# Attention over 96 units: the value products of two units side by side, and one copy of VectorE moved

## The chip, the cores and the metric

One core of a Trainium2 chip runs the whole layer as a single program. The metric is the time of one execution on the device in microseconds. Besides the DMA queues four engines do the work: TensorE (PE, with its weight loads PEld), VectorE (DVE), ScalarE (ACT) and GpSimd (POOL). Each runs its own list of instructions in order, and they wait for each other by semaphores.

## The reference

The reference is one layer of an encoder, on 1024 sample tokens and 512 prompt tokens. The change lies in the attention, of which there are two kinds with 8 heads of 64 each:

```python
# windowed, with a sink, per block of 128 queries and up to 3 blocks of keys
s = einsum(q, k) * HEAD_DIM ** -0.5           # masked to |i - j| <= 128
m = max(max(s), sink);  p = exp(s - m)
o = einsum(p / (sum(p) + exp(sink - m)), v)
# neighbourhood, 2-D, with a bias per relative position
s = einsum(q, k) * HEAD_DIM ** -0.5 + bias    # masked to the neighbourhood
o = einsum(softmax(s), v)
```

After it come a norm, the output projection, a router and 16 experts with SwiGLU.

## The kernel before, in words

The attention is the function `attend`. It works through 24 blocks of 128 queries: 12 of the windowed kind and 12 of the neighbourhood kind, mostly in turn. A block has four pairs of heads; a block and a pair are a **unit**, so there are 96 units. A unit has 384 keys in 16 of the blocks (64 units) and 256 keys in the other 8 (32 units).

A unit goes through a pipeline over several **steps**; each engine runs its own loop over u from 0 to 100, and in step u it works on different units:

- TensorE: scores of unit u for both heads (L886); then the probabilities of unit u-2 are transposed into `flip_ps` (L896, 4 small transposes per 128 keys); then the output of unit u-5 is transposed into `out_ps` (L907); and last the values of unit u-3 are multiplied into `mixed_ps` (L927), both heads beside each other in two halves of the array. All are fp32, so that a matmul is recorded as two.
- VectorE: for each head of unit u the mask or bias is added to the scores and their maximum taken (L809, the two **additions**); the maximum of both is negated (L817 or L820); for unit u-2 the reciprocal of the sum (L825) and the copy of one half of the transposed probabilities to `at_flipped` (L830, the **copy**); for unit u-5 the output is scaled by the reciprocal and written to `ld_out` (L845, the **scaling**).
- ScalarE: the copy of `mixed_ps` for unit u-4 to `at_o_turn` (L744, the **output copy**); the copy of the other half of the transposed probabilities of unit u-2 (L750); and the exponentials of unit u, one per head (L758).

Buffers are few, and the waits for them set the order: three banks for scores, one bank for `mixed_ps` (so the values of a unit wait until the output copy of the unit before has read it: `o_copied`), and one buffer `out_ps` for the turned output (so the turn of one unit waits until the scaling of the unit before has read it: `scaled`). SyncE moves biases and values in, and outputs out. In the last steps ScalarE also squares the first tile of outputs that has come back from memory (L767), for the stage that follows.

Of the kernel before, what the change touches and what calls it, by code (L numbers as in the profile page):

```python
# [24 lines left out]
ACT = mybir.ActivationFunctionType  # L25
# [3 lines left out]
P = 128  # L29
# [9 lines left out]
HD = 64  # L39
# [585 lines left out]
def attend(nc, d, keep, shared, lead):  # L625
# [4 lines left out]
    with ctx:  # L630
# [40 lines left out]
        def flip_from(v, i):  # L671
            tiles = units[v][0].keys // P
            return flip_ps[i][:, 0:2 * tiles * HD].rearrange("p (h c q) -> p h c q", h=2, q=HD)
# [62 lines left out]
        @block.scalar  # L736
        def _(act):
            for u in range(STEPS):
                v = u - WEIGH
                if 0 <= v < N:  # L740
                    act.wait_ge(weighed, v + 1)
                    if v >= 2:
                        act.wait_ge(o_turned, v - 1)
                    act.activation(o_turn[:, v % 2, :], mixed_ps[:, 0:P], ACT.Copy).then_inc(o_copied, 1)  # L744
                if 0 <= u - FLIP < N:
                    v = u - FLIP
                    act.wait_ge(flipped_ps, 2 * v + 1)
                    if 2 * v >= FLIPS:
                        act.wait_ge(weighed, v - FLIPS // 2 + 1)
                    act.activation(flip_to(v, 0), flip_from(v, 0), ACT.Copy).then_inc(copied[0], 1)  # L750
                if u < N:
                    b, r = units[u][0], u % STATS
                    act.wait_ge(bounded, u + 1)
                    if u >= PROBS // 2:
                        act.wait_ge(flipped_ps, 2 * (u - PROBS // 2) + 2)
                    pair, n = units[u][1], b.keys + b.window
                    for h in range(2):
                        act.activation(probs[:, (2 * u + h) % PROBS, 0:n],  # L758
                                       raw[:, 2 * pair + h, NEAR_KEYS - b.keys:NEAR_KEYS - b.keys + n],
                                       ACT.Exp, bias=neg_top[:, r, h:h + 1],  # L760
                                       accum_out=sums[:, r, h:h + 1]).then_inc(exped, 1)

                if u == N - 1 or u == N:
                    k = u - (N - 1)
                    if k == 0:
                        act.wait_ge(lead.o_in[0], 16)
                    act.activation(lead.merged[:, k * HALF:(k + 1) * HALF], lead.o[0][:, k * HALF:(k + 1) * HALF],  # L767
                                   ACT.Square, accum_out=lead.ss[:, k:k + 1]).then_inc(lead.squared, 1)
                if u == N + 2:
                    act.wait_ge(lead.squared, 2)  # L770
                    act.activation(lead.rt[:], lead.ss[:], ACT.Sqrt, bias=shared.eps[:],
                                   scale=1.0 / HALF).then_inc(lead.root, 1)

            def split(j):
                act.wait_ge(lead.w_in[j], 16)
                act.activation(lead.w_hi[j], lead.w[:, j, :], ACT.Copy,
                               scale=shared.gain_out[:, j:j + 1]).then_inc(lead.hi_w, 1)

            split(0)
            act.wait_ge(lead.refined, REFINE)  # L780
            for k in range(2):
                c = slice(k * HALF, (k + 1) * HALF)
                act.activation(lead.merged[:, c], lead.o[0][:, c], ACT.Copy,
                               scale=lead.rs[:, k:k + 1]).then_inc(lead.normed, 1)
            split(1)
            for k in range(2):
                act.wait_ge(lead.turned, k + 1)
                act.activation(lead.m_hi[:, 4 * k:4 * k + 4, :].rearrange("p j c -> p (j c)"), lead_ps[k][:],
                               ACT.Copy).then_inc(lead.hi_m, 1)

        @block.vector
        def _(dve):
            dve.wait_ge(shared.later_in, 48)
            dve.tensor_scalar(neg_sink[:], sink[:], -1.0, None, ALU.mult).then_inc(negated, 1)
            dve.tensor_copy(raw[:, :, NEAR_KEYS:], sink[:].unsqueeze(2)).then_inc(negated, 1)
            dve.wait_ge(negated, 2)
            for u in range(STEPS):
                if u < N:
                    b, pair, bi = units[u]
                    r = u % STATS  # L800
                    if not b.window and pair == 0:
                        dve.wait_ge(bias_in[b.number % BIASES], 16 * (b.number // BIASES + 1))
                    for h in range(2):
                        dve.wait_ge(scored, 2 * u + h + 1)
                        if b.window:
                            add = band[:, b.mask_at:b.mask_at + b.keys]
                        else:
                            add = bias[:, b.number % BIASES, 2 * pair + h, 0:b.keys]
                        dve.tensor_tensor_reduce(out=raw[:, 2 * pair + h, NEAR_KEYS - b.keys:NEAR_KEYS],  # L809
                                                 in0=score[(2 * u + h) % SCORES][:, 0:b.keys], in1=add, scale=1.0, scalar=-3.0e38,  # L810
                                                 op0=ALU.add, op1=ALU.max,
                                                 accum_out=top[:, r, h:h + 1]).then_inc(added, 1)
                    dve.wait_ge(added, 2 * u + 2)
                    if b.window:

                        mine = neg_sink[:, 2 * pair:2 * pair + 2]
                        dve.scalar_tensor_tensor(out=neg_top[:, r, :], in0=top[:, r, :], scalar=-1.0, in1=mine,  # L817
                                                 op0=ALU.mult, op1=ALU.min).then_inc(bounded, 1)
                    else:
                        dve.tensor_scalar(neg_top[:, r, :], top[:, r, :], -1.0, None,  # L820
                                          ALU.mult).then_inc(bounded, 1)
                if 0 <= u - FLIP < N:
                    v, r = u - FLIP, (u - FLIP) % STATS
                    dve.wait_ge(exped, 2 * v + 2)
                    dve.reciprocal(rden[:, r, :], sums[:, r, :]).then_inc(inverted, 1)  # L825

                    dve.wait_ge(flipped_ps, 2 * v + 2)
                    if 2 * v >= FLIPS:
                        dve.wait_ge(weighed, v - FLIPS // 2 + 1)
                    dve.tensor_copy(flip_to(v, 1), flip_from(v, 1)).then_inc(copied[1], 1)  # L830
                if u >= OUT:
                    v, r = u - OUT, (u - OUT) % STATS
                    b, pair, bi = units[v]
                    dve.wait_ge(o_turned, v + 1)
                    dve.wait_ge(inverted, v + 1)
                    if pair == 0 and bi >= O_SLOTS:

                        dve.wait_ge(stored[bi % O_SLOTS], 16 * (bi // O_SLOTS))
                    if b.window:
                        dst = o[:, bi % O_SLOTS, :].rearrange("p (h c e) -> p h c e", h=2, c=PAIRS)[:, :, pair, :]  # L840
                    else:
                        dst = o[:, bi % O_SLOTS, pair * P:(pair + 1) * P].rearrange("p (h e) -> p h e", h=2)

                    own = out_ps[:, :, 0:HD]
                    dve.tensor_tensor(dst, own,  # L845
                                      rden[:, r, :].unsqueeze(2).broadcast_to([P, 2, HD]),
                                      ALU.mult).then_inc(scaled, 1)
                if u == N + 3:
                    dve.wait_ge(lead.root, 1)
                    inverse_root(dve, lead.refined, 0, lead.ss[:], lead.rt[:], [lead.tmp[:, i, :] for i in range(3)],  # L850
                                 lead.rs[:], 1.0 / HALF)
# [17 lines left out]
        def _(pe):  # L869

            for u in range(STEPS):
# [30 lines left out]
                if u >= OUT:  # L902
# [4 lines left out]
                    turned = [nc.tensor.transpose(out_ps[:, h, 0:HD], o_turn[ROWS[h], v % 2, :],  # L907
                                                  ident[ROWS[h], ROWS[h]]) for h in range(2)]
                    turned[1].then_inc(o_turned, 1)
                for v in (u - WEIGH + 1,):  # L910
                    if 0 <= v < N:
                        b, pair, bi = units[v]
                        if not b.window and pair == 0:
                            pe.wait_ge(v_in[b.strip % 2], 16 * len(V_TILES) * (b.strip // 2 + 1))
                        if v >= 1:
                            pe.wait_ge(o_copied, v)
                        for h in range(2):
                            pe.wait_ge(copied[h], v + 1)
# [1 line left out]
                        for i in range(tiles):  # L920
                            for h in range(2):
                                if b.window:
                                    values = keep.v.tiles(b.first_key + i, 1)[:, 0, h * HD:(h + 1) * HD]
                                else:
                                    slot = (len(V_TILES) * b.strip + b.v_tiles[i]) % V_SLOTS
                                    values = v_near[:, slot, pair * P + h * HD:pair * P + (h + 1) * HD]
                                last = nc.tensor.matmul(mixed_ps[h * HD:(h + 1) * HD, 0:P], values,  # L927
                                                        flipped[:, (2 * v + h) % FLIPS, i * P:(i + 1) * P],
                                                        start=i == 0, stop=i == tiles - 1, tile_position=(0, h * HD))
                        last.then_inc(weighed, 1)  # L930
# [1129 lines left out]
```

## Time and profile before

| | us |
|---|---|
| median of 3 runs | 2554.14 (2553.98 to 2557.11) |
| the profiled execution's own time | 2556.15 |
| its span | 2554.4 |
| TensorE busy, of the span | 2462.6 |
| attention: first scores to last scaling | 327.4 to 541.6 |

TensorE is busy in 96% of the span, but that is a mean: in the attention it is the engine with most to do, beside VectorE and ScalarE that are busy for more than 80% of the time each. The experts, from about 760 us on, are most of the span and TensorE fills them. A row of the timeline merges neighbouring instructions of one kind; a bracket at its end tells how long its engine sat idle before, and who released it.

### The profile page before, as it was taken

How to read it: one execution, taken by the hardware profiler on the slowest of the kernel's cores; microseconds unless marked ns; L12 is line 12 of the kernel's file. 1: busy time of each engine (PE TensorE's matmuls, PEld its weight loads, DVE VectorE, ACT ScalarE, POOL GpSimd, SP SyncE). 2: the span in 40 equal slices, each digit the busy share in tenths (PEclk: the TensorE clock that was granted, in tenths of full speed). 3: DMA queues.
4: the chain of work that ended last, by engine and by line, in shares of the span. 5: the costliest groups of instructions: out<-in, count | busy, mean ns of one | idle time of the engine just before them, and what ended most of it. 6: DMA issues, size and time to landing. Idle time of an engine off the chain costs nothing.

```text
span 2554.4 us, 42578 instructions
## 1 busy us (share of the span) xinstructions
PE 2462.6 (96%) x16082; PEld 2204.3 (86%) x16082; DVE 1683.9 (66%) x2550; ACT 1475.4 (58%) x2081; POOL 159.2 (6%) x165
## 2 busy tenths in 40 slices
PE   8999999989949999999999999999999999999997
PEld 7888866667739899998989999898999989999896
DVE  6354278864577676666767667676766767676676
ACT  4333278877636555565655656555565655556574
POOL 0000000000010101010110101011010100101010
PEclk9999999989969999999999999999999999999999
DMA  5343254454437767676776767677676767767685
GB/s 186 111 140 112 66 176 133 138 188 143 146 143 256 241 241 252 218 258 227 253 242 242 245 227 253 225 258 244 237 243 229 255 223 257 245 233 249 229 320 212
DMA packets 99668, 542.37 MB, mean 212 GB/s; under 512 B 11072, under 2 KB 15552, under 8 KB 49408
## 3 DMA queue, kind: packets, MB, share of 16 engines
q1 hardware_dynamic: 92192, 515.30, 57.2%
q0 software_dynamic: 7392, 25.96, 4.5%
q8 instruction: 52, 0.85, 0.1%
q14 instruction: 32, 0.26, 0.0%
HBM read 500.32 MB, written 40.89 MB: 212 GB/s over the span
## 4 chain that ended last, share of the span: by engine, by line
PE 68%; DVE 2%; DMA 1%; ACT 1%; issue 0%; POOL 0%; DVEq 0%; SPq 0%; ACTq 0%; POOLq 0%
PE ex_gate_ps L1854 16%; PE ex_up_ps L1854 15%; PE ex_gate_ps L1856 7%; PE ex_up_ps L1856 7%; PE ex_up_ps L1868 2%; PE ex_down_ps L1868 2%; PE ex_down_ps L1869 2%; PE ex_down_ps L1870 2%; PE ex_down_ps L1871 2%; PE ex_up_ps L1870 2%; PE ex_down_ps L1872 2%; PE ex_up_ps L1872 2%; PE ex_up_ps L1869 2%; PE ex_up_ps L1871 2%; PE ex_turn_ps L1829 1%; PE ex_turn_ps L1831 0%
## 5 line engine op out<-in xcount | busy, mean ns | idle before, releaser
L1706 DVE TENSOR_TENSOR ex_w_lo<-ex_w,ex_w_hi 128x2048 fp32r<-128x2048 f32 x384 | 880.0, 2292 | 461.0 <-ACT ex_w_hi L1623 448.5
L1623 ACT ACTIVATE ex_w_hi<-ex_w 128x2048 fp32r<-128x2048 f32 x384 | 733.4, 1910 | 221.4 <-PE ex_down_ps L1872 106.9
L1854 PE MATMUL ex_gate_ps<-ex_xt,ex_w_hi 128*128 128x384 f32 x2048 | 594.2, 360 | 1.5 <-DVE ex_xt L1712 1.5
L1854 PE MATMUL ex_up_ps<-ex_xt,ex_w_hi 128*128 128x384 f32 x2048 | 592.1, 359 | 0.0
L1856 PE MATMUL ex_gate_ps<-ex_xt,ex_w_lo 128*128 128x192 f32 x2048 | 513.7, 251 | 0.0
L1856 PE MATMUL ex_up_ps<-ex_xt,ex_w_lo 128*128 128x192 f32 x2048 | 512.7, 250 | 0.0
L1856 PEld LDWEIGHTS ex_gate_ps<-ex_xt,ex_w_lo 128*128 128x128 f32 x2048 | 392.5, 192 | 0.6
L1856 PEld LDWEIGHTS ex_up_ps<-ex_xt,ex_w_lo 128*128 128x128 f32 x2048 | 391.2, 191 | 0.0
L1854 PEld LDWEIGHTS ex_gate_ps<-ex_xt,ex_w_hi 128*128 128x128 f32 x2048 | 385.8, 188 | 2.3 <-issue 1.7
L1854 PEld LDWEIGHTS ex_up_ps<-ex_xt,ex_w_hi 128*128 128x128 f32 x2048 | 384.4, 188 | 0.0
L1641 ACT ACTIVATE ex_gate_low<-ex_gate_ps 128x384 f32<-128x384 f32 x128 | 62.9, 491 | 208.4 <-PE ex_gate_ps L1856 207.1
L1643 ACT ACTIVATE ex_up_low<-ex_up_ps 128x384 f32<-128x384 f32 x128 | 62.8, 491 | 208.0 <-PE ex_up_ps L1856 208.0
L423 DVE TENSOR_TENSOR pj_w_lo<-pj_w,pj_w_hi 128x1024 fp32r<-128x1024 f32 x54 | 66.2, 1225 | 155.0 <-ACT pj_w_hi L343 154.7
L758 ACT ACTIVATE at_probs<-at_raw,at_neg_top 128x385 f32<-128x385 f32 (+3 forms) x192 | 110.0, 574 | 29.2 <-DVE at_neg_top L820 14.3
L1564 POOL DMA_INDIRECT acc_scratch<-ex_y_s,ex_scatter_s x15 | 24.2, 1612 | 1436.9 <-DVE ex_y_p L1749 1436.9
L1733 DVE TENSOR_TENSOR ex_up_sum<-ex_up_ps,ex_up_low 128x384 f32<-128x384 f32 x128 | 71.4, 557 | 50.5 <-ACT ex_up_low L1643 50.5
L1868 PE MATMUL ex_down_ps<-ex_w_hi,ex_ht 128*128 128x512 f32 x256 | 101.4, 396 | 0.0
L1868 PE MATMUL ex_up_ps<-ex_w_hi,ex_ht 128*128 128x512 f32 x256 | 101.3, 396 | 0.0
L1869 PE MATMUL ex_down_ps<-ex_w_lo,ex_ht 128*128 128x512 f32 x256 | 99.8, 390 | 0.0
L1871 PE MATMUL ex_down_ps<-ex_w_hi,ex_ht 128*128 128x512 f32 x256 | 99.8, 390 | 0.0
L1870 PE MATMUL ex_down_ps<-ex_w_hi,ex_ht 128*128 128x512 f32 x256 | 99.8, 390 | 0.0
L1870 PE MATMUL ex_up_ps<-ex_w_hi,ex_ht 128*128 128x512 f32 x256 | 99.7, 389 | 0.0
(316 smaller groups left out, 4056.1 us busy)
## 6 DMA issues: line engine op xcount, KB each, us to landing
ex_w<-in_w_experts SPq DMA_DIRECT2D x384, 1024.0 KB, 4.8
pj_w<-in_w_in SPq DMA_DIRECT2D x54, 512.0 KB, 3.6
at_bias<-in_near_bias SPq DMA_DIRECT2D x8, 1536.0 KB, 8.2
at_v_near<-v_scratch SPq DMA_DIRECT2D x24, 256.0 KB
o_scratch<-ld_out SPq DMA_DIRECT2D x24, 256.0 KB, 4.5
q_p<-in_x SPq DMA_DIRECT2D x12, 512.0 KB, 4.3
acc_scratch<-k_p SPq DMA_DIRECT2D x12, 512.0 KB, 5.1
h_scratch<-q_p SPq DMA_DIRECT2D x12, 512.0 KB, 2.9
```

What stands on the lines that cost most here:

```text
L423: dve.tensor_tensor(w_lo[:, i % W_SLOTS, :, :].rearrange("p j c -> p (j c)"), w[:, i % W_SLOTS, :], w_hi[:, i % W_SLOTS, :, :].rearrange(" ...
L758: act.activation(probs[:, (2 * u + h) % PROBS, 0:n], raw[:, 2 * pair + h, NEAR_KEYS - b.keys:NEAR_KEYS - b.keys + n], ACT.Exp, bias=neg_to ...
L1623: act.activation(w_hi[:, c % SLOTS, :], w[:, c % SLOTS, :], ACT.Copy).then_inc(hi_w, 1)
L1706: dve.tensor_tensor(w_lo[:, c % SLOTS, :], w[:, c % SLOTS, :], w_hi[:, c % SLOTS, :].bitcast(F32), ALU.subtract).then_inc(lo_w, 1)
L1733: dve.tensor_tensor(up_sum[:], up_ps[:, :, 0:CAP], up_low[:], ALU.add).then_inc(up_summed, 1)
L1854: nc.tensor.matmul(out[:, b, 0:2 * CAP], w_hi[:, slot, f], xt[:, k, :, :].rearrange("p h c -> p (h c)"), start=k == 0, stop=False)
L1856: last = nc.tensor.matmul(out[:, b, 0:CAP], w_lo[:, slot, f], xt[:, k, 0, :], start=False, stop=k == DT - 1)
L1868: nc.tensor.matmul(out[0], s_hi, hi, start=start, stop=False)
L1869: nc.tensor.matmul(out[0], s_hi, lo, start=False, stop=False)
L1870: nc.tensor.matmul(out[0], s_lo, hi, start=False, stop=stop)
L1871: nc.tensor.matmul(out[1], both, hi, start=start, stop=False)
L1872: last = nc.tensor.matmul(out[1], both, lo, start=False, stop=stop)
```

## The change

In every even step TensorE multiplies the values of two units, u-4 and u-3, one after the other into two ranges of columns of the one bank `mixed_ps`; in odd steps it multiplies none. ScalarE copies both outputs with one instruction, twice as wide, in every odd step. And in every odd step VectorE's copy of the transposed probabilities stands between the additions of the two heads, in place of behind the reciprocal. The last steps, which have no scores, keep the copy where it was.

```diff
+                if u % 2 and u > WEIGH:
+                    v = u - WEIGH - 1
+                    act.wait_ge(weighed, v + 2)
                     if v >= 2:
-                        act.wait_ge(o_turned, v - 1)
-                    act.activation(o_turn[:, v % 2, :], mixed_ps[:, 0:P], ACT.Copy).then_inc(o_copied, 1)
+                        act.wait_ge(o_turned, v)
+                    act.activation(o_turn[:].rearrange("p u c -> p (u c)"), mixed_ps[:, 0:2 * P],
+                                   ACT.Copy).then_inc(o_copied, 2)
...
+            def copy_turned(v):
+                dve.wait_ge(flipped_ps, 2 * v + 2)
+                if 2 * v >= FLIPS:
+                    dve.wait_ge(weighed, v - FLIPS // 2 + 1)
+                dve.tensor_copy(flip_to(v, 1), flip_from(v, 1)).then_inc(copied[1], 1)
...
+                        if h == 0 and u % 2 and u >= FLIP:
+                            copy_turned(u - FLIP)
...
-                    dve.tensor_copy(flip_to(v, 1), flip_from(v, 1)).then_inc(copied[1], 1)
+                    if u % 2 == 0 or u >= N:
+                        copy_turned(v)
...
-                for v in (u - WEIGH + 1,):
+                for v in (u - WEIGH, u - WEIGH + 1) if u % 2 == 0 else ():
...
-                        if v >= 1:
+                        if v >= 2 and v % 2 == 0:
                             pe.wait_ge(o_copied, v)
...
-                                last = nc.tensor.matmul(mixed_ps[h * HD:(h + 1) * HD, 0:P], values,
+                                last = nc.tensor.matmul(mixed_ps[h * HD:(h + 1) * HD, v % 2 * P:(v % 2 + 1) * P], values,
```

TensorE's list in the middle of the attention, before (two steps of 384 keys):

```order
L886 MATMUL at_score<-k_s,q_s 128x384 x2
L896 MATMUL at_flip<-ident,at_probs 128x64 x12
L907 MATMUL at_out<-ident,at_o_turn 128x64 x2
L927 MATMUL at_mixed<-at_flipped,v_s 64x128 x6
L886 MATMUL at_score<-k_s,q_s 128x384 x2
L896 MATMUL at_flip<-ident,at_probs 128x64 x12
L907 MATMUL at_out<-ident,at_o_turn 128x64 x2
L927 MATMUL at_mixed<-at_flipped,v_s 64x128 x6
```

and of the change, an odd step and the even one behind it:

```order
L894 MATMUL at_score<-k_s,q_s 128x384 x2
L904 MATMUL at_flip<-ident,at_probs 128x64 x12
L915 MATMUL at_out<-ident,at_o_turn 128x64 x2
L894 MATMUL at_score<-k_s,q_s 128x384 x2
L904 MATMUL at_flip<-ident,at_probs 128x64 x12
L915 MATMUL at_out<-ident,at_o_turn 128x64 x2
L935 MATMUL at_mixed<-at_flipped,v_s 64x128 x12
```

The six value matmuls of an odd step have moved behind those of the even step; between the turned outputs (`at_out`) of the two steps there are now only scores and transposes.

VectorE's list before, one step of a neighbourhood block from its first addition to its scaling (each L809 has a second row for its accumulator):

```order
L809 ISA at_raw,at_top<-at_score,at_bias 128x384
L809 ISA at_top 128x1
L809 ISA at_raw,at_top<-at_score,at_bias 128x384
L809 ISA at_top 128x1
L820 TENSOR_SCALAR at_neg_top<-at_top 128x2
L825 RECIPROCAL at_rden<-at_sums 128x2
L830 COPY at_flipped<-at_flip 128x6x64
L845 TENSOR_TENSOR ld_out<-at_out,at_rden 128x2x64
```

and the same piece in an odd step of the change:

```order
L817 ISA at_raw,at_top<-at_score,at_bias 128x384
L817 ISA at_top 128x1
L803 COPY at_flipped<-at_flip 128x6x64
L817 ISA at_raw,at_top<-at_score,at_bias 128x384
L817 ISA at_top 128x1
L830 TENSOR_SCALAR at_neg_top<-at_top 128x2
L835 RECIPROCAL at_rden<-at_sums 128x2
L853 TENSOR_TENSOR ld_out<-at_out,at_rden 128x2x64
```

The copy has moved ahead of the second addition; the scaling still stands behind the same seven instructions.

## Rows read from the trace of the kernel before

**Rows 1.** Stretches of the attention: columns us, then each engine's busy time, PEclk, DMA.
```profile
360.00:400.00 40.00, 37.26 (x524) 26.74 (x522) 33.69 (x149) 33.01 (x110) 0.00 (x0) 1.00 0.45 154
...
535.00:540.00 5.00, 4.62 (x38) 3.13 (x38) 0.92 (x3) 3.51 (x10) 0.00 (x0) 0.50 0.95 267
```

**Rows 2.** Waits from 327 to 541 us: waiter, releaser, us in total, times, longest.
```profile
PE at_mixed L927 <- ACT at_o_turn L744: 13.4, 39, 2.3
...
PE at_out L907 <- DVE ld_out L845: 0.5, 1, 0.5
```

**Rows 3.** Timeline of TensorE, 384 keys: start us, us, engine, line, operation.
```profile
365.21 0.92 PE L886 MATMUL at_score<-k_s,q_s 64*128 64x384 f32 x4
365.96 0.54 PE L896 MATMUL at_flip<-ident,at_probs 64*128 64x64 f32 x12
366.33 0.23 PE L907 MATMUL at_out<-ident,at_o_turn 64*128 64x64 f32 x2
366.49 0.88 PE L927 MATMUL at_mixed<-at_flipped,at_v_near 128*64 128x128 f32 x12
367.30 0.92 PE L886 MATMUL at_score<-k_s,q_s 64*128 64x384 f32 x4
...
368.43 0.25 PE L907 MATMUL at_out<-ident,at_o_turn 64*128 64x64 f32 x2
368.95 0.88 PE L927 MATMUL at_mixed<-at_flipped,v_s 128*64 128x128 f32 x12 [0.27 <-ACT at_o_turn L744]
369.76 0.92 PE L886 MATMUL at_score<-k_s,q_s 64*128 64x384 f32 x4
```

**Rows 4.** Timeline of VectorE in the same stretch.
```profile
366.16 0.56 DVE L809 CUSTOM_DVE_ANT_0 at_raw<-at_score,band 128x384 f32<-128x384 f32 x1 [0.50 <-PE at_score L886]
366.64 0.55 DVE L809 CUSTOM_DVE_ANT_0 at_raw<-at_score,band 128x384 f32<-128x384 f32 x1
...
367.24 0.16 DVE L817 SCALAR_TENSOR_TENSOR at_neg_top<-at_top,at_neg_sink 128x2 f32<-128x2 f32 x1
...
367.39 0.54 DVE L830 COPY at_flipped<-at_flip 128x384 f32<-128x384 f32 x1
367.84 0.28 DVE L845 TENSOR_TENSOR ld_out<-at_out,at_rden 128x128 f32<-128x128 f32 x1
```

**Rows 5.** Timeline of ScalarE in the same stretch.
```profile
367.43 0.62 ACT L758 ACTIVATE at_probs<-at_raw,at_neg_top 128x385 f32<-128x385 f32 x1 [0.41 <-DVE at_neg_top L817]
...
368.64 0.25 ACT L744 ACTIVATE at_o_turn<-at_mixed 128x128 f32<-128x128 f32 x1
368.80 0.48 ACT L750 ACTIVATE at_flipped<-at_flip 128x384 f32<-128x384 f32 x1
```

**Rows 6.** Timeline of TensorE: scores twelve steps apart.
```profile
404.67 0.92 PE L886 MATMUL at_score<-k_s,q_s 64*128 64x384 f32 x4
...
432.31 0.70 PE L886 MATMUL at_score<-k_s,q_s 64*128 64x256 f32 x4
```

**Rows 7.** Timeline of TensorE and VectorE, 256 keys.
```profile
447.30 0.70 PE L886 MATMUL at_score<-k_p,q_p 64*128 64x256 f32 x4
448.03 0.42 DVE L809 CUSTOM_DVE_ANT_0 at_raw<-at_score,band 128x256 f32<-128x256 f32 x1 [0.25 <-PE at_score L886]
...
448.54 0.66 PE L927 MATMUL at_mixed<-at_flipped,at_v_near 128*64 128x128 f32 x8 [0.24 <-ACT at_o_turn L744]
449.13 0.70 PE L886 MATMUL at_score<-k_p,q_p 64*128 64x256 f32 x4
449.32 0.28 DVE L845 TENSOR_TENSOR ld_out<-at_out,at_rden 128x128 f32<-128x128 f32 x1
```

**Rows 8.** Groups by line and form: TensorE's weight loads for the turned outputs; busy, mean ns.
```profile
L907 PEld LDWEIGHTS at_out<-ident,at_o_turn 64*128 64x128 f32 x192 | 15.1, 141 | 1.3 <-issue 0.7 <-ACT at_o_turn L744 0.6
```

**Rows 9.** Timeline of ScalarE at the end of the attention.
```profile
534.34 0.63 ACT L767 ACTIVATE ld_merged<-ld_o 128x512 f32<-128x512 f32 x1 [1.24 <-DMA ld_o<-o_scratch]
...
540.53 1.15 ACT L776 ACTIVATE ld_w_hi<-q_s,gain_out 128x1024 fp32r<-128x1024 f32 x1 [0.26 <-DMA q_s<-in_w_out]
```

More of the change, by code:

```diff
@@ L738, in _ @@
             for u in range(STEPS):
-                v = u - WEIGH
-                if 0 <= v < N:
-                    act.wait_ge(weighed, v + 1)
+                if u % 2 and u > WEIGH:
+                    v = u - WEIGH - 1
+                    act.wait_ge(weighed, v + 2)
                     if v >= 2:
-                        act.wait_ge(o_turned, v - 1)
-                    act.activation(o_turn[:, v % 2, :], mixed_ps[:, 0:P], ACT.Copy).then_inc(o_copied, 1)
+                        act.wait_ge(o_turned, v)
+                    act.activation(o_turn[:].rearrange("p u c -> p (u c)"), mixed_ps[:, 0:2 * P],
+                                   ACT.Copy).then_inc(o_copied, 2)
                 if 0 <= u - FLIP < N:
@@ L825, in _ @@
                     dve.reciprocal(rden[:, r, :], sums[:, r, :]).then_inc(inverted, 1)
-                    dve.wait_ge(flipped_ps, 2 * v + 2)
-                    if 2 * v >= FLIPS:
-                        dve.wait_ge(weighed, v - FLIPS // 2 + 1)
-                    dve.tensor_copy(flip_to(v, 1), flip_from(v, 1)).then_inc(copied[1], 1)
+                    if u % 2 == 0 or u >= N:
+                        copy_turned(v)
                 if u >= OUT:
```

## The prediction

> **What bounds the kernel now.** I began with the page's busy shares: TensorE 96% of the span, so only time that TensorE loses counts. The change touches the attention alone, so I cut the span into stretches. There all three engines are loaded [rows 1]: in 40 us TensorE is busy 37.26, VectorE 33.69, ScalarE 33.01, at a granted clock of 1.00. No engine is full, so what ends a step must be a ring of waits. The list of waits names one: the values wait for ScalarE's output copy, 39 times, 13.4 us by TensorE's matmuls [rows 2]. The timeline shows that steps come in pairs. An even one (365.21 to 367.30, 2.09 us) has no gap; the odd one (367.30 to 369.76, 2.46 us) holds its values back until 368.95 [rows 3]. The ring of a pair, from even scores to even scores: scores to first addition 0.95 (366.16 - 365.21), to the second 0.48, to the exponentials 0.79 (367.43 - 366.64), both exponentials 1.21 (368.64 - 367.43), output copy to values 0.31, values to scores 0.81 [rows 3 to 5]. The sum is 4.55, exactly the pair. Over twelve steps a pair takes (432.31 - 404.67) / 6 = 4.61 [rows 6], the first and the fourth step of a neighbourhood block being a little longer; I take 4.59 as the mean of the 32 pairs with 384 keys. The 16 pairs with 256 keys take 2 x 1.83 = 3.66 [rows 7].
>
> **What the change removes.** The values of an even step now need an output copy that ScalarE made in the odd step before, so the ring above has a whole step more and is no bound: 4.55 us of work in three steps. One ScalarE instruction of about 0.25 us [rows 5] goes from each pair; the wide one that stays costs between 0.25 (128 columns) and 0.48 (384 columns) [rows 5], I take 0.37. ScalarE is not the bound, so this alone is worth nothing.
>
> TensorE without waits would need, per pair: even step 0.75 to the transposes, 0.37 to the turned output, 0.16 to the values [rows 3], then two sets of values. Three key tiles cost 0.81 up to the next scores [rows 3], two cost 0.59 [rows 7], so a tile is 0.22, and six are 0.81 + 0.66 = 1.47 (bounds: 0.65 and 0.81 for the second set). The odd step is 0.75 + 0.37 + 0.16 = 1.28. Together 2.75 + 1.28 = 4.03. So there are 0.56 us a pair to be had if nothing else waits.
>
> **What becomes late next.** Three new chains.
>
> First, the moved copy. The transposes of the even step follow those of the odd one after only 1.28 us, and need VectorE's copy of the odd step's. In its new place it starts 0.95 + 0.48 = 1.43 after the odd scores and ends at 1.97; those transposes are due at 1.28 + 0.75 = 2.03. It is just in time. In its old place it would end at 0.95 + 1.23 + 0.54 = 2.72 (367.39 - 366.16 = 1.23 [rows 4]) and the pair would be some 0.7 us longer. Thus the second edit pays for the first, and no more. Its price is that the second addition and the exponentials of odd units are 0.45 us later (copy to next instruction 367.84 - 367.39 [rows 4]; up to 0.54 if an addition can't overlap it).
>
> Second, the scaling, which I take as the new bound. The turned output of a step needs the scaling of the step before, since `out_ps` is a single buffer. Before, that wait ended last only once [rows 2]: the odd step's turn stood at 368.43, the even step's scaling ended at 367.84 + 0.28 = 368.12 [rows 3, 4]. Now the even step's turned output is due only 1.28 + 1.12 = 2.40 after the odd scores, but the odd step's scaling still stands behind both additions, the small instructions and the copy, which make the same sum in either order: 367.84 - 366.16 = 1.68 [rows 4]. The ring, from odd scores to odd scores: 0.95 to the addition, 1.68 to the scaling, 0.28 for it, 0.06 to release TensorE (ScalarE's output copy ends at 368.89, the values start at 368.95 [rows 3, 5]), turned output to values 0.16, two sets of values 1.47. The sum is 4.60, against 4.59 before. So the wait changes its name and its place (from the values to the turned output of the even step) and nearly keeps its size. Queued behind it on TensorE are both sets of values and the next scores, for which all three engines wait.
>
> I add 0.05 for what a stalled TensorE has not prepared; its lower bound is 0 (a stalled set of values takes the same 0.81 as a free one [rows 3]), its upper bound two exposed weight loads of 0.14 [rows 8]. So 4.65. With 256 keys: 0.73 + 1.29 + 0.28 + 0.06 + 0.16 + 1.03 = 3.55 (448.03 - 447.30; 449.32 - 448.03; values 0.59 + 2 x 0.22 [rows 7]), plus 0.05: 3.60.
>
> VectorE's instructions overlap by 0.09 us: the copy of 0.54 is followed after 0.45 [rows 4]. The Trainium skill (VectorE: DVE Perf Modes, "The DRAIN you can't avoid") says that the next operation can't issue until the pipe is empty, but that one that is not held starts earlier. By its first half the ring would be 0.09 longer and the kernel 48 x 0.09 = 4.3 us slower than my sum; the row is of the second half, and I keep 0.45.
>
> Third, ScalarE's ring over two pairs: odd scores, addition 0.95, 0.48, copy 0.45, to the exponentials 0.79, exponentials 1.21, ScalarE's own copy 0.39 (0.48 less the same overlap), exponentials 1.21, wide output copy 0.37 + 0.06, turned output 0.16 to the scores, even step 2.75. That is 8.82, or 4.41 a pair. It is shorter than 4.60, so it doesn't decide, though it is still a bound should the scaling be none.
>
> **Beginning and end.** The first pair of values comes a step later, while TensorE waits for VectorE in any case: nothing. At the end ScalarE waits for tile 0 from memory (1.24 us) and later for the output weights (540.53) [rows 9]. Transfers end this stage: I count no gain there, and up to 1 us either way. What follows starts when the attention ends, and moves with it whole.
>
> **Sum.** 32 x (4.65 - 4.59) = +1.9; 16 x (3.60 - 3.66) = -1.0; together +0.9 us. On the profiled execution's own 2556.15 that is 2557.1. The median of the runs is 2.0 lower, which gives 2555.0.
>
> **Rivals.**
> - *The scaling is no bound; ScalarE's ring is (4.41).* For it: removing the wait was worth a whole step, and the release may come sooner than I read. Against: all terms of the scaling's ring but the release stand in rows. Gain 32 x 0.18 = 5.8, and at the same 4% 16 x 0.15 = 2.4: 2556.15 - 8.2 - 2.0 = 2546.0.
> - *TensorE runs without gaps (4.03).* Gain 32 x 0.56 = 17.9, and 16 x 0.49 = 7.8 at the same 12%: 2528. Against it: both rings.
> - *Slower: the stall at the turned output exposes weight loads.* The two turned matmuls and the first values behind them each find weights not loaded, since the loads are queued behind the same wait: 2 x 0.14 [rows 8]. The pair is 4.60 + 0.28 = 4.88 and 3.83: 32 x 0.29 + 16 x 0.17 = +12.0, so 2566. It decides from a pair that is 0.11 longer than before (4.70 and 3.77), which is 5 us over 48 pairs. For it: this wait stands right ahead of loads. Against: the stalled values of before show no such cost.
> - *Slower by the clock.* Gaps of 0.3 us leave the clock at 1.00; at the end of the attention, after a wait of up to 2.3 us, it is 0.50, that is 1.2 instead of 2.4 GHz [rows 1, 2]. Gaps here would be 0.6 us a pair in place of 0.4. Were that enough, 4.03 us of matmuls would double and the kernel be over 100 us slower. The Trainium skill (TensorE: Matmul & The Clock Gate, "A second HAM failure mode: psum-queue depth-cycling") tells of a kernel in which frequent short idles between groups of matmuls made the clock swing; the rows at 0.4 us a pair show none.
>
> **How the numbers follow.** Forecast (a pair between 4.53 and 4.77) 0.63; ScalarE's ring 0.20; exposed loads 0.13; no gaps 0.03; clock 0.01. A difference under 0.2%, 5.1 us, is about what a measurement of this kernel can't tell from none. Of the forecast's 0.63, 0.03 lie below that and 0.05 above; of ScalarE's ring nearly all is faster. Faster 0.25, same 0.57, slower 0.18. The range reaches down to ScalarE's ring, 2545, and up to 2563, inside the exposed loads.
>
> **What would show it.** In the profile after: the wait of `at_mixed` for `at_o_turn` gone; `at_out` waiting for `ld_out` some 0.4 us in each even step, about 20 us in all; even scores following odd ones after 1.3 to 1.5 us, odd ones following even ones after some 3.2; transposes not waiting for VectorE's copy; clock 1.00. If `at_out` waits for `at_o_turn` instead, in odd steps, and pairs take 4.4 us, the first rival is right. If pairs take 4.6 with no wait at the turned output, or if the attention is as long as before and the time is not, I am wrong.

## The result, and the profile after

The changed kernel takes 2561.32 us (median of 8 runs, 2558.35 to 2563.47) against 2554.55 us before (8 runs): the ratio is 1.0022, with a 95% interval of 1.0012 to 1.0033. It is slower by 3 to 8 us. The forecast was 2555.0 in a range of 2545 to 2563, with no measurable change, a difference under 0.2%, as the likeliest case (0.57) and slower at 0.18. The time lies in the range, 6.3 us above the forecast and at its slower edge. The kernel is slower beyond the noise. The prediction's line of 0.2% lies inside the interval, and the measured 0.22% is just past it, on the side of the less likely case.

In the profiled executions (2559.04 us here, 2556.15 before) the attention takes the difference. From the first scores to the scores of the last unit it was 530.25 - 327.43 = 202.8 us and is 534.21 - 326.96 = 207.3. Its tail up to the first matmul of the next stage was 17.7 and is 17.2. From that matmul to the end of the span it was 2554.4 - 547.97 = 2006.4 and is 2557.3 - 551.38 = 2005.9.

The list of waits from 327 to 545 us (waiter, releaser, us in total, times, longest) has a new name in the place of the values' wait [rows 2]:

```profile
PE at_out L915 <- DVE ld_out L853: 10.2, 37, 0.5
...
PEld at_out L915 <- ACT at_o_turn L744: 6.4, 16, 0.8
...
PE at_out L915 <- ACT at_o_turn L744: 3.5, 10, 0.5
```

The turned output of the even steps now waits for VectorE's scaling, 37 times, where it did so once before. That is 0.28 us each on average by this list. Stretches of the attention (us, busy time of each engine, PEclk, DMA), beside [rows 1]:

```profile
360.00:400.00 40.00, 37.74 (x508) 30.07 (x505) 31.35 (x140) 31.17 (x99) 0.00 (x0) 1.00 0.44 150
535.00:540.00 5.00, 2.81 (x46) 2.04 (x42) 3.04 (x14) 4.08 (x13) 0.00 (x0) 1.00 0.69 234
```

TensorE's busy time went up a little (37.74 for 37.26) although each pair takes longer: the busy share does not tell which of two orders is faster. The clock stayed at 1.00.

TensorE's timeline of an odd step and the even one behind it (start us, us, engine, line, operation), beside [rows 3]. In all that follows, "odd scores" are the scores of an odd step, and a ring is a loop of waits that comes back to the same instruction one pair of steps later:

```profile
367.02 0.92 PE L894 MATMUL at_score<-k_s,q_s 64*128 64x384 f32 x4
367.77 0.53 PE L904 MATMUL at_flip<-ident,at_probs 64*128 64x64 f32 x12
368.20 0.28 PE L915 MATMUL at_out<-ident,at_o_turn 64*128 64x64 f32 x2
368.31 1.19 PE L894 MATMUL at_score<-k_s,q_s 64*128 64x384 f32 x4
369.11 0.76 PE L904 MATMUL at_flip<-ident,at_probs 64*128 64x64 f32 x12
370.08 0.28 PE L915 MATMUL at_out<-ident,at_o_turn 64*128 64x64 f32 x2 [0.21 <-DVE ld_out L853]
370.29 1.53 PE L935 MATMUL at_mixed<-at_flipped,v_s 128*64 128x128 f32 x24
371.75 0.92 PE L894 MATMUL at_score<-k_s,q_s 64*128 64x384 f32 x4
```

and VectorE's in the odd step, beside [rows 4]:

```profile
367.97 0.56 DVE L817 CUSTOM_DVE_ANT_0 at_raw<-at_score,band 128x384 f32<-128x384 f32 x1 [0.89 <-PE at_score L894]
...
368.45 0.56 DVE L803 COPY at_flipped<-at_flip 128x384 f32<-128x384 f32 x1
368.92 0.55 DVE L817 CUSTOM_DVE_ANT_0 at_raw<-at_score,band 128x384 f32<-128x384 f32 x1
...
369.51 0.16 DVE L827 SCALAR_TENSOR_TENSOR at_neg_top<-at_top,at_neg_sink 128x2 f32<-128x2 f32 x1
369.59 0.16 DVE L835 RECIPROCAL at_rden<-at_sums 128x2 f32<-128x2 f32 x1
369.67 0.27 DVE L853 TENSOR_TENSOR ld_out<-at_out,at_rden 128x128 f32<-128x128 f32 x1
```

The turned output comes 0.43 us behind the transposes in the odd step (368.20 - 367.77) and 0.97 behind them in the even one (370.08 - 369.11). So it is held for 0.54 us. The list of waits shows about half of that, since it counts from the recorded end of the transposes, and those are recorded with 0.76 us here for 0.53 in the odd step.

From odd scores to odd scores it is 371.75 - 367.02 = 4.73 us. It is 4.71 to 4.81 in 23 of the 30 pairs whose two steps have 384 keys; the others, at the start or behind blocks of 256 keys, are shorter. Before, the mean was 4.59. The ring can be read off: scores to first addition 0.95, to the scaling 1.70, the scaling 0.27 (it ends at 369.94), to the turned output 0.14, to the values 0.21, two sets of values 1.46. The sum is 4.73. A pair of 256 keys takes 3.67 us, against 3.65.

### The profile page after: what moved, and what is told of

Read it like the earlier page. It is cut to its first block, busy times and chain, and to the rows that moved or that the text cites. A ratio compares the mean times of both kernels' runs of the same rounds, so it can differ in the third digit from the quotient of the medians.

```text
span 2557.3 us, 42484 instructions
## 1 busy us (share of the span) xinstructions
PE 2467.1 (96%) x16082; PEld 2223.1 (87%) x16082; DVE 1680.2 (66%) x2550; ACT 1468.2 (57%) x2033; POOL 162.3 (6%) x165
## 4 chain that ended last, share of the span: by engine, by line
PE 68%; DVE 2%; DMA 1%; ACT 1%; issue 0%; POOL 0%; DVEq 0%; SPq 0%; ACTq 0%; POOLq 0%
PE ex_gate_ps L1862 16%; PE ex_up_ps L1862 15%; PE ex_gate_ps L1864 7%; PE ex_up_ps L1864 7%; PE ex_up_ps L1876 2%; PE ex_down_ps L1876 2%; PE ex_down_ps L1877 2%; PE ex_down_ps L1878 2%; PE ex_down_ps L1879 2%; PE ex_up_ps L1878 2%; PE ex_down_ps L1880 2%; PE ex_up_ps L1880 2%; PE ex_up_ps L1877 2%; PE ex_up_ps L1879 2%; PE ex_turn_ps L1837 1%; PE ex_turn_ps L1839 0%
```

## Experiments

The times are medians of 5 to 11 runs. The kernel before had 2554.55 us beside the changed one (as above), 2555.48 us (16 runs) beside the first four experiments (pairing alone to scaling early) and 2555.10 (18 runs) beside the other four. "Pair" is the steady length of two steps with 384 keys in the profile.

| kernel | us | ratio to before (95%) | pair, us |
|---|---|---|---|
| before | 2554.6 to 2555.5 | 1 | 4.59 |
| changed | 2561.3 | 1.0022 (1.0012 to 1.0033) | 4.73 |
| pairing alone | 2564.6 | 1.0036 (1.0023 to 1.0048) | 4.86 |
| moved copy alone | 2574.0 | 1.0070 (1.0056 to 1.0084) | 5.02 |
| values ahead of the turned output | 2545.0 | 0.9958 (0.9944 to 0.9972) | 4.35 |
| scaling early | 2549.3 | 0.9978 (0.9969 to 0.9987) | 4.48 |
| two banks for the turned output | 2553.1 | 0.9993 (0.9984 to 1.0002) | 4.55 |
| its control with one bank | 2561.5 | 1.0027 (1.0017 to 1.0038) | 4.75 |
| values ahead, copy late | 2565.1 | 1.0037 (1.0024 to 1.0051) | 4.86 |
| values ahead, two narrow output copies | 2542.4 | 0.9950 (0.9937 to 0.9964) | 4.30 |

### Each half of the change by itself

The pairing alone, with VectorE's copy behind the reciprocal in every step:

```diff
-                        if h == 0 and u % 2 and u >= FLIP:
-                            copy_turned(u - FLIP)
...
-                    if u % 2 == 0 or u >= N:
-                        copy_turned(v)
+                    copy_turned(v)
```

> The values of two units together, VectorE's copy where it stood (behind the reciprocal) in every step. Theory (the copy's old place makes the even step's transposes late, the scaling is the next wait behind them): odd scores to the end of the copy 0.95 + 1.23 + 0.54 = 2.72, transposes 0.1 later, turned output 0.43, values 0.21, scores 1.46: a pair of 384 keys takes some 4.9 us against 4.73 in the changed kernel, and the kernel some 7 to 12 us more than it: about 2570. Rival (only the scaling decides, since it ends last in either order: its sum is the same): pairs of 4.73 us and 2561.

Measured: 2564.6 us and pairs of 4.86. The timeline shows the ring that decides: odd scores, end of VectorE's copy at 389.27 + 0.54 = 389.81, transposes of the even step 0.10 later, odd scores again 2.04 after that:

```profile
387.09 0.92 PE L891 MATMUL at_score<-k_s,q_s 64*128 64x384 f32 x4
...
389.27 0.54 DVE L803 COPY at_flipped<-at_flip 128x384 f32<-128x384 f32 x1
...
389.91 0.59 PE L901 MATMUL at_flip<-ident,at_probs 64*128 64x64 f32 x12 [0.55 <-issue]
...
391.95 0.70 PE L891 MATMUL at_score<-k_p,q_p 64*128 64x256 f32 x4
```

The first theory holds in the pair's length to 0.04 us. The time is not as expected: 5 us under its figure, and 3.3 us more than the changed kernel where 7 to 12 were expected. I had applied the loss to all pairs: with 256 keys a pair is 3.69, 0.02 over the changed kernel's.

The moved copy alone, in the kernel before:

```diff
+                        if h == 0 and u % 2 and u >= FLIP:
+                            copy_turned(u - FLIP)
...
-                    dve.tensor_copy(flip_to(v, 1), flip_from(v, 1)).then_inc(copied[1], 1)
+                    if u % 2 == 0 or u >= N:
+                        copy_turned(v)
```

> The kernel before with VectorE's copy between the additions in odd steps; the values stay one unit to a step. Theory (the kernel before is bound by exponentials, output copy, values; later exponentials of odd units open a second such ring): 0.95 + 0.48 + 0.45 + 0.79 + 1.21 + 0.31 + 0.81 = 5.00 us a pair against 4.59, with 256 keys some 0.3 more: +18 us, about 2572. Rival (the odd units' exponentials have slack, so the move is free by itself): no change, 2554.5.

Measured: 2574.0 us, 18.5 more than before, and a pair of 378.79 - 373.77 = 5.02:

```profile
373.77 0.92 PE L893 MATMUL at_score<-k_s,q_s 64*128 64x384 f32 x4
...
374.38 0.62 ACT L758 ACTIVATE at_probs<-at_raw,at_neg_top 128x385 f32<-128x385 f32 x1 [0.88 <-DVE at_neg_top L826]
...
375.59 0.25 ACT L744 ACTIVATE at_o_turn<-at_mixed 128x128 f32<-128x128 f32 x1
...
375.90 0.88 PE L934 MATMUL at_mixed<-at_flipped,v_s 128*64 128x128 f32 x12 [0.78 <-ACT at_o_turn L744]
...
376.70 0.92 PE L893 MATMUL at_score<-k_s,q_s 64*128 64x384 f32 x4
...
378.79 0.92 PE L893 MATMUL at_score<-k_s,q_s 64*128 64x384 f32 x4
```

The values of the even step (375.90) wait for ScalarE's output copy (375.59), which stands behind the odd unit's late exponentials (374.38). The wait of the kernel before is there with two and a half times its size:

```profile
PE at_mixed L934 <- ACT at_o_turn L744: 33.6, 47, 0.9
```

So VectorE's copy was not free to move, and neither half pays alone: the pairing costs 9.1 us, the copy's move 18.5, both together 6 to 7.

### Taking the values out of the ring

Only the order of two pieces of TensorE's list is turned round in each step:

```diff
-                if u >= OUT:
-                    v = u - OUT
-                    pe.wait_ge(o_copied, v + 1)
-                    if v >= 1:
-                        pe.wait_ge(scaled, v)
-                    turned = [nc.tensor.transpose(out_ps[:, h, 0:HD], o_turn[ROWS[h], v % 2, :],
-                                                  ident[ROWS[h], ROWS[h]]) for h in range(2)]
-                    turned[1].then_inc(o_turned, 1)
                 for v in (u - WEIGH, u - WEIGH + 1) if u % 2 == 0 else ():
...
                         last.then_inc(weighed, 1)
+                if u >= OUT:
+                    v = u - OUT
+                    pe.wait_ge(o_copied, v + 1)
+                    if v >= 1:
+                        pe.wait_ge(scaled, v)
+                    turned = [nc.tensor.transpose(out_ps[:, h, 0:HD], o_turn[ROWS[h], v % 2, :],
+                                                  ident[ROWS[h], ROWS[h]]) for h in range(2)]
+                    turned[1].then_inc(o_turned, 1)
```

> The changed kernel, but in each step TensorE turns the output of unit u-5 behind the values and not ahead of them. Theory (the changed kernel's pair is the ring scores, additions, scaling, turned output, two sets of values): the values no longer stand behind the wait for the scaling, the next ring is ScalarE's (exponentials of both steps, wide output copy), 4.4 to 4.5 us a pair against 4.73, with 256 keys about 0.2 less: 10 us less than the changed kernel, about 2551, below the kernel before as well; at_out waits for ld_out no more. Rival (what costs is the pairing itself: exposed weight loads, two sets of values in one bank, copies twice as wide): the pair stays at 4.7 us and the kernel at 2561.

Measured: 2545.0 us, 10.5 under the kernel before and 16 under the changed one. Two successive pairs take 4.35 us each on average (an even step of 2.74 and an odd one of 1.57 or 1.65):

```profile
370.27 0.86 PE L894 MATMUL at_score<-k_s,q_s 64*128 64x384 f32 x4
370.98 0.53 PE L904 MATMUL at_flip<-ident,at_probs 64*128 64x64 f32 x12
371.44 1.53 PE L927 MATMUL at_mixed<-at_flipped,v_s 128*64 128x128 f32 x24
372.90 0.27 PE L936 MATMUL at_out<-ident,at_o_turn 64*128 64x64 f32 x2
373.01 0.86 PE L894 MATMUL at_score<-k_s,q_s 64*128 64x384 f32 x4
373.71 0.54 PE L904 MATMUL at_flip<-ident,at_probs 64*128 64x64 f32 x12
...
374.14 0.36 ACT L744 ACTIVATE at_o_turn<-at_mixed 128x256 f32<-128x256 f32 x1
...
374.55 0.28 PE L936 MATMUL at_out<-ident,at_o_turn 64*128 64x64 f32 x2 [0.30 <-ACT at_o_turn L744]
...
374.66 0.86 PE L894 MATMUL at_score<-k_s,q_s 64*128 64x384 f32 x4
```

Behind the transposes the values start at once (371.44), and when they are done the scaling of the step before has long ended. The wait of `at_out` for `ld_out` is gone from the list. What waits now is the odd step's turned output, for ScalarE:

```profile
PEld at_out L936 <- ACT at_o_turn L744: 21.3, 47, 0.8
...
PE at_out L936 <- ACT at_o_turn L744: 14.4, 41, 0.6
```

That is the third chain of the prediction, ScalarE's ring over two pairs, foretold at 4.41 for the case that the scaling does not bind. The expectation of about 2551 was 6 us too high. Against the changed kernel a pair of 384 keys lost 0.38 and one of 256 keys 0.27 (3.40 for 3.67), more than it had for either: 32 x 0.38 + 16 x 0.27 = 16.5 us.

### Making the scaling earlier

```diff
                             copy_turned(u - FLIP)
+                    if u % 2 and u >= OUT:
+                        scale_turned(u)
                     dve.wait_ge(added, 2 * u + 2)
...
-                if u >= OUT:
+                if u >= OUT and (u % 2 == 0 or u >= N):
+                    scale_turned(u)
```

`scale_turned` holds the scaling's code unchanged.

> The changed kernel, but in odd steps VectorE's scaling stands between the second addition and the negation of the maxima, in place of behind the reciprocal. Theory (scaling ring): the scaling starts 0.48 instead of 0.76 us after the second addition's start, the ring shrinks from 4.73 to 4.45; the exponentials of odd units are 0.1 to 0.2 later, which ScalarE's ring over two pairs spreads to under 0.1 a pair (about 4.5): 7 to 9 us less than the changed kernel, about 2553. Rival (exponentials of odd units decide): the pair gets 0.1 to 0.2 longer, about 2566.

Measured: 2549.3 us, pairs of 4.48. VectorE's rows show what the new place costs, and TensorE's what it gives:

```profile
369.34 0.92 PE L899 MATMUL at_score<-k_s,q_s 64*128 64x384 f32 x4
...
371.24 0.55 DVE L835 CUSTOM_DVE_ANT_0 at_raw<-at_score,at_bias 128x384 f32<-128x384 f32 x1
...
371.71 0.29 DVE L819 TENSOR_TENSOR ld_out<-at_out,at_rden 128x128 f32<-128x128 f32 x1
371.92 0.16 DVE L850 TENSOR_SCALAR at_neg_top<-at_top 128x2 f32<-128x2 f32 x1
371.98 0.16 DVE L855 RECIPROCAL at_rden<-at_sums 128x2 f32<-128x2 f32 x1
...
372.14 0.28 PE L920 MATMUL at_out<-ident,at_o_turn 64*128 64x64 f32 x2
...
373.81 0.92 PE L899 MATMUL at_score<-k_s,q_s 64*128 64x384 f32 x4
```

The scaling starts 0.47 behind the second addition, and the negation comes 0.68 behind it in place of 0.59: VectorE has to wait there for the addition's result anyway, and the scaling fills most of that gap. The kernel beats both the kernel before and the changed one by this alone, with TensorE's order that of the change.

The scaling's ring is shorter, but not gone. The turned output of the even step still starts 0.14 behind the scaling's end (372.14 - 372.00), and from odd scores to odd scores the ring's terms still add up to the pair: 2.37 to the scaling, 0.29, 0.14, and 1.67 to the next odd scores, 4.47. It was 4.73, so the link was shortened by 0.26 and the pair with it. ScalarE's ring is about as long here: in odd steps the turned output waits for `at_o_turn` 42 times. The expectation of about 2553 was 4 us too high; a pair of 256 keys takes 3.43 for 3.67, and 32 x 0.25 + 16 x 0.24 = 11.8 us are what was measured (12.0).

### A second buffer for the turned output

`out_ps` has two banks, one for each head. One transpose for both heads needs only one of them, so the other is free for the next unit:

```diff
-                    own = out_ps[:, :, 0:HD]
+                    own = out_ps[:, v % 2, 0:P].rearrange("p (h e) -> p h e", h=2)
...
-                    if v >= 1:
-                        pe.wait_ge(scaled, v)
-                    turned = [nc.tensor.transpose(out_ps[:, h, 0:HD], o_turn[ROWS[h], v % 2, :],
-                                                  ident[ROWS[h], ROWS[h]]) for h in range(2)]
-                    turned[1].then_inc(o_turned, 1)
+                    if v >= 2:
+                        pe.wait_ge(scaled, v - 1)
+                    nc.tensor.transpose(out_ps[:, v % 2, 0:P], o_turn[:, v % 2, :], ident[:]).then_inc(o_turned, 1)
```

> The changed kernel with a second buffer for the turned output: both heads are turned by one transpose of 128 columns in place of two of 64, and the units take the two banks of out_ps by turns, so that a turn waits for the scaling of the unit two before. Order and everything else as in the changed kernel. Theory (single buffer and scaling): at_out no longer waits for ld_out, the ring of 4.73 us is gone and ScalarE's ring over two pairs is next, 4.4 to 4.5 us a pair: 2546 to 2551. Rival (it was the order on TensorE, values ahead of the turned output, that gained in the run before, by other means than this wait): no gain, 2561.

The control has the same single transpose, but `out_ps[:, 0, 0:P]` for every unit and the wait of the change.

> The control of the run with two buffers: the changed kernel with one transpose of 128 columns for both heads, but a single bank and the waits of the changed kernel. Expected by the theory: the ring through the scaling stays and its term from turned output to values changes by up to 0.1 us either way: a pair of 4.7 to 4.85, 2560 to 2566. If this run is as fast as the one with two buffers, the form of the transpose and not the buffer is what gains.

Measured: 2553.1 with two banks (not clear of the kernel before, 0.9984 to 1.0002), 2561.5 with one; the pairs are 4.55 and 4.75. TensorE's rows with two banks, from the turned output of an even step (373.17), which waits for nobody:

```profile
373.17 0.33 PE L915 MATMUL at_out<-ident,at_o_turn 128*128 128x128 f32 x1
373.43 1.53 PE L933 MATMUL at_mixed<-at_flipped,v_s 128*64 128x128 f32 x24
374.89 0.92 PE L894 MATMUL at_score<-k_s,q_s 64*128 64x384 f32 x4
...
376.51 0.92 PE L894 MATMUL at_score<-k_s,q_s 64*128 64x384 f32 x4
```

and with one bank, where it waits (375.20):

```profile
372.14 0.92 PE L894 MATMUL at_score<-k_s,q_s 64*128 64x384 f32 x4
...
375.20 0.30 PE L915 MATMUL at_out<-ident,at_o_turn 128*128 128x128 f32 x1 [0.21 <-DVE ld_out L853]
375.43 1.53 PE L933 MATMUL at_mixed<-at_flipped,v_s 128*64 128x128 f32 x24
376.89 0.59 PE L894 MATMUL at_score<-k_s,q_s 64*128 64x384 f32 x2
```

In the ring through the scaling the form of the transpose costs nothing measurable (4.75 for 4.73), and the buffer is worth 8.5 us. It is worth less than the other order. By the sum (no run separates the two) the reason is that the transpose of 128 columns takes longer than two of 64 side by side (0.26 to 0.25 up to what stands behind it, for 0.11 to the scores and 0.16 to the values), in both steps, and both lie in ScalarE's ring. The expectation of 2546 to 2551 had left that out and was 2 us too low.

### The copy's place once more, and the width of the output copy

Values ahead of the turned output, but the copy behind the reciprocal (the diff of the pairing alone):

> The kernel with the values ahead of the turned output, but VectorE's copy behind the reciprocal in every step, as before the change. Theory (without the scaling's ring the copy's place is worth its full price): odd scores to the end of the copy 2.72, transposes 0.10 later (389.81 to 389.91 in the run with the pairing alone), 0.39 and 0.19 and 1.46 as there: 4.86 us a pair, as in that run, about 2564, near 20 us more than with the copy between the additions (2545). Rival (the copy's move matters only together with the scaling's wait): below 2550.

Measured: 2565.1 us and 4.86, as in the pairing alone. With the copy late, the order on TensorE is worth nothing; with the copy early, it is worth 16 us (2561.3 to 2545.0). Of the three rings (copy, scaling, ScalarE) the longest that is left standing sets the pair.

Values ahead, and two output copies of 128 columns:

```diff
-                    act.activation(o_turn[:].rearrange("p u c -> p (u c)"), mixed_ps[:, 0:2 * P],
-                                   ACT.Copy).then_inc(o_copied, 2)
+                    for w in range(2):
+                        act.activation(o_turn[:, w, :], mixed_ps[:, w * P:(w + 1) * P],
+                                       ACT.Copy).then_inc(o_copied, 1)
```

> The kernel with the values ahead of the turned output, but ScalarE copies the outputs of the two units with two instructions of 128 columns again, one behind the other. Theory (ScalarE's ring over two pairs: exponentials, output copy, turned output in the odd step): the first unit's output is free 0.12 us earlier (0.25 for 0.37), which gives back up to 0.06 a pair; its own copy and the exponentials start 0.04 later. From 2545 to about 2543 to 2545. Rival (ScalarE is bound by its instructions' number): 2 to 4 us slower.

Measured: 2542.4 us, pairs of 4.30, the fastest kernel of the study. It is 12.7 us under the kernel before, where values ahead with one wide copy was 10.5 under it; these two were not run beside each other. The rows of an odd step (the two copies are one row):

```profile
373.91 0.42 ACT L745 ACTIVATE at_o_turn<-at_mixed 128x128 f32<-128x128 f32 x2
...
374.22 0.27 PE L937 MATMUL at_out<-ident,at_o_turn 64*128 64x64 f32 x2 [0.20 <-ACT at_o_turn L745]
```

From the start of ScalarE's copying to the turned output it is 0.31 here and 0.41 with the wide instruction (374.55 - 374.14). The unit that is needed first does not wait for the other's columns. That is 0.10 once in the ring over two pairs, or the 0.05 a pair that was gained.

The pair lengths account for the times. With 32 pairs of 384 and 16 of 256 keys, the changes of the pairs come to +19 us for the moved copy alone (4.59 to 5.02, 3.65 to 3.97; measured +18.5), -12 for the values ahead (3.40; -10.5), +5 for the change (3.67; +5.8 to +6.8). The whole attention in the profiles, from the first scores to those of the last unit, agrees for all eight. Against the 202.8 us before, the pairing alone has +8.2, the moved copy alone +18.6, the values ahead -11.5, the scaling early -6.3, two banks -2.8, the control +5.3, the values ahead with the copy late +8.6 and two narrow copies -13.4. Each is within 1.4 us of the difference of the medians.

## Why the prediction was right, and where it was off

**The bound before** was read rightly. Its ring foretold 5.00 us a pair for the moved copy alone, and 5.02 was measured.

**The removed wait** went as described: `at_mixed` waits for `at_o_turn` no more.

**The moved copy pays for the pairing and no more:** only in part. The transposes of the even step, due at 2.03 after the odd scores, start at 2.09 (369.11 - 367.02), 0.10 behind the copy's end at 369.01. So the copy is not "just in time" but holds them 0.06 us; the prediction had counted no release there. It costs nothing, as the scaling's wait ends later. In its old place the copy was said to make the pair some 0.7 longer; by the runs the pair is 4.86 instead of 4.35 with the values ahead, so 0.51, but only 4.86 instead of 4.73 in the order of the change. There the move gives back 3 us of the 9 that the pairing costs, since the scaling's ring stands right behind the copy's.

**The scaling as the new bound:** right in kind, shown by two edits that each take one of its links out (order, buffer), by one that shortens a link by 0.26 us and the pair with it (place), and by a control that leaves all in. Its ring was put at 4.60, and 0.05 added for the stall. The sign that `at_out` would wait about 20 us in all came out at 10.2 in the list; by the starts in the timeline the hold is 0.54 us a pair, and the prediction's own rows gave 0.57 (0.95 + 1.68 + 0.28 + 0.06 - 2.40). Odd scores follow even ones mostly after 3.44 to 3.48 us, not after "some 3.2"; its own sum gave 4.65 - 1.28 = 3.37.

**The term that was mis-sized** is what a stalled TensorE adds, 0.05 of the sum. Two parts of it are in the rows. The release: I took 0.06 from ScalarE's output copy [rows 3, 5]; behind VectorE's scaling it is 0.14 to 0.15 in all 37 waits of the profile, 0.10 behind VectorE's copy. And turned output to values is 0.21 there, where unstalled it was 0.16 [rows 3] (with the pairing alone it is 0.18 to 0.19, also unstalled). Together they are 0.13 over the ring of 4.60, and 0.08 over the 0.05 that was allowed: 48 x 0.08 = 3.8 us. With it the sum would have been +4.7 us and not +0.9; the medians differ by 6.8, with 3.1 as the interval's lower end. So a size was off and not the mechanism. That the time still lay in the range is owed to its reach of 8 us upward, which the prediction took from the rival below and not from the doubt about this term.

**The rival of exposed weight loads** had the right place and twice the size (0.28). The prediction let it decide from a pair of 4.70 and 3.77, and let its own forecast reach up to 4.77, so that the two overlap: 4.73 fits both, the 3.67 of 256 keys only the forecast. What speaks against its mechanism is that the same two turned matmuls, with the same weight loads behind the same kind of wait, start only 0.05 to 0.06 us after the end of ScalarE's copy (374.55 - 374.50 with the values ahead, and in each of the 10 waits for `at_o_turn` of the changed kernel). So the 0.08 of the release goes with who releases and not with the loads. Of the other 0.05, turned output to values, a part can be the loads; no run separates it.

**The rival of ScalarE's ring** did not come about in the changed kernel, but its 4.41 was within 0.06 of the 4.35 that appears as soon as the scaling is out of the way.

**The clock:** 1.00 throughout the steady part, as forecast.

**What stays open:** the two profiles explain 3 to 5 of the 6.8 us between the medians. The changed kernel's profiled execution (2559.04) is 2.3 us under its median and that of the kernel before (2556.15) is 1.6 over its own, so the profiles show a smaller difference than the runs. The rest is within the interval and its cause was not looked for. Why TensorE starts later behind VectorE than behind ScalarE is open too.

## What to carry to other kernels

Before two pieces of work are put together, list what now comes sooner after what: here the turn of the output came 0.8 us sooner behind a scaling that had not moved, and a single buffer that had 0.3 us of slack became the bound. Write the ring of waits as a sum of rows, and do the same for the next two rings, since the one that is removed gives at most the distance to the next. When a ring goes through a wait, look what stands in the queue behind it: putting work that needs nothing ahead of the waiting instruction was worth 16 us here, more than a second buffer with the transpose that it needed. And take the latency of a release from the engine that will release.

## What the runs showed of the hardware

- In the changed kernel TensorE starts 0.14 to 0.15 us after the recorded end of VectorE's scaling (37 waits), and 0.05 to 0.06 after that of ScalarE's output copy (10 waits, for the same kind of matmul). With the pairing alone it starts 0.09 to 0.11 after the end of VectorE's copy (42 waits).
- VectorE's addition behind the copy starts 0.47 after it (368.92 - 368.45) with a copy of 0.56: the two overlap by 0.09, as in [rows 4].
- At the end of the attention the granted clock was 0.50 before from 535 to 540 us, behind the 2.3 us in which TensorE waited for ScalarE. In the changed kernel it is 1.00 there, 0.95 from 540 to 545 and 0.50 from 545 to 550, with TensorE idle for 3.8 us (542.82 to 546.65). What the later fall is worth no run shows; the tail is 0.5 us shorter, and in it ScalarE waits 2.8 us for the output weights.
